# Weight sums added by GpSimd from two plain loads, and seven-product quads in two FFN down groups

## What is computed

```python
g = h2 @ w_gate;  u = h2 @ w_up              # 1024 -> 2816
x = x + (silu(g) * u) @ w_down               # first block's FFN
y = square(relu(h @ w_up)) @ w_down          # the two MLPs, 1024 -> 4096 -> 1024
mod = silu(c) @ ada_w + ada_b                # 112 rows of 128 values
```

## Time and profile before

| | us |
|---|---|
| median of 3 runs (lowest, highest) | 1738.54 (1738.35, 1739.76) |
| the profiled execution | 1739.29 |
| its span in the trace | 1737.4 |
| TensorE busy | 1713.6 |
| VectorE busy | 1254.3 |
| ScalarE busy | 685.2 |
| GpSimd busy | 120.1 |

### The profile page before, as it was taken

One profiled execution on the slowest core, in us unless ns is written; L12 is line 12 of the kernel. 1 busy time (PEld: TensorE's weight loads), 2 busy tenths in 40 slices (PEclk: granted clock), 3 DMA queues, 4 the chain that ended last, 5 costly groups with the idle time before them and its releaser, 6 DMA issues. The chain is left out here.

```text
span 1737.4 us, 23695 instructions
## 1 busy us (share of the span) xinstructions
PE 1713.6 (99%) x9000; PEld 1431.2 (82%) x9000; DVE 1254.3 (72%) x1869; ACT 685.2 (39%) x1051; POOL 120.1 (7%) x182
## 2 busy tenths in 40 slices
PE   9999999999999999999999999999999999999998
PEld 8777777888888888888898989887767889898987
DVE  7866555766666676877886868678675887777766
ACT  5236544322222253234544343344534453434341
POOL 0000000011011000100200000002000010000001
PEclk9999999999999999999999999999999999999999
DMA  7321112666566533653264646431411336364541
GB/s 253 106 97 38 43 55 67 199 207 229 193 206 229 193 110 112 234 179 118 63 178 126 183 131 185 166 121 49 139 49 40 107 94 172 98 170 107 163 167 49
DMA packets 67299, 235.77 MB, mean 136 GB/s; under 512 B 7808, under 2 KB 9984, under 8 KB 67008
## 3 DMA queue, kind: packets, MB, share of 16 engines
q1 hardware_dynamic: 46800, 161.24, 27.4%
q0 software_dynamic: 20112, 72.62, 15.2%
q10 hardware_dynamic: 288, 0.59, 0.1%
HBM read 231.55 MB, written 2.10 MB: 134 GB/s over the span
## 5 line engine op out<-in xcount | busy, mean ns | idle before, releaser
L1347 DVE TENSOR_TENSOR w_lo<-w_raw,w_hi 128x1024 fp32r<-128x1024 f32 x307 | 375.2, 1222 | 104.8 <-ACT w_hi L925 98.0
L925 ACT ACTIVATE w_hi<-w_raw 128x1024 fp32r<-128x1024 f32 x307 | 322.3, 1053 | 308.7 <-PE psum L2270 142.7
L2268 PE MATMUL psum<-h_hi,w_hi 128*128 128x512 f32 x1056 | 411.8, 390 | 0.0
L2269 PE MATMUL psum<-h_lo,w_hi 128*128 128x512 f32 x1056 | 410.9, 389 | 0.0
L2270 PE MATMUL psum<-h_hi,w_lo 128*128 128x512 f32 x1056 | 410.8, 389 | 0.0
L2268 PEld LDWEIGHTS psum<-h_hi,w_hi 128*128 128x128 f32 x1056 | 198.3, 188 | 41.7 <-issue 0.5
L2270 PEld LDWEIGHTS psum<-h_hi,w_lo 128*128 128x128 f32 x1056 | 198.2, 188 | 41.3
L2269 PEld LDWEIGHTS psum<-h_lo,w_hi 128*128 128x128 f32 x1056 | 198.3, 188 | 41.3 <-issue 0.5
L1358 DVE SCALAR_TENSOR_TENSOR ada_raw<-ada_raw,c_row 128x1024 f32<-128x1024 f32 x112 | 136.0, 1219 | 5.8 <-DMA ada_raw<-in_ada 5.8
L2268 PE MATMUL psum<-hid_hi,w_hi 128*128 128x512 f32 x344 | 133.8, 389 | 0.0
L2269 PE MATMUL psum<-hid_lo,w_hi 128*128 128x512 f32 x344 | 133.8, 389 | 0.0
(11 more groups left out here) (376 smaller groups left out, 2875.5 us busy)
## 6 DMA issues: line engine op xcount, KB each, us to landing
w_raw<-in_wstream SPq DMA_DIRECT2D x283, 512.0 KB, 4.1
ada_raw<-in_ada POOLq DMA_DIRECT2D x112, 512.0 KB, 4.0
w_diff<-in_wstream SPq DMA_DIRECT2D x12, 512.0 KB, 5.8
w_raw<-in_wstream POOLq DMA_DIRECT2D x12, 512.0 KB, 5.5
w_diff<-in_wstream POOLq DMA_DIRECT2D x12, 512.0 KB, 5.4
x<-in_xT SPq DMA_DIRECT2D x8, 256.0 KB, 5.4
outT<-x SPq DMA_DIRECT2D x16, 128.0 KB, 1.8
con<-in_consts SPq DMA_DIRECT2D x1, 1032.0 KB, 9.5
```

Source lines behind the costliest of these rows:

```text
L925: act.activation(w_hi[:, slot, :], w_raw[:, slot, :], ACT.Copy).then_inc(whi_done, 1)
L1347: dve.tensor_tensor(w_lo[:, slot, :], w_raw[:, slot, :], w_hi[:, slot, :].bitcast(F32), ALU.subtract).then_inc(wlo_done, 1)
L2268: pe.matmul(bank, w_hi[:, slot, w], hi[:, ra + k, :], start=k == 0, stop=False)
L2269: pe.matmul(bank, w_hi[:, slot, w], lo[:, ra + k, :], start=False, stop=False)
```

## The change

The sums A and D are added by GpSimd instructions: SyncE loads a21 into the slot and a22 into a new buffer w_part, GpSimd adds them (`first_sum`); SyncE loads only a21 into w_diff, and GpSimd adds a11, which lies in its ring slot anyway (`last_sum`). The slot of a11 is held until then (diff_made). Groups 0 and 1 of the FFN get quads on x, and their gate/up stages make the pair sums. Rows: the FFN's gate/up stages 13, 20, 13; each quads stage with rows has 2, one per quad behind unit D; the first MLP's up stages 0, 8, 8, 7. In a stage ahead of quads the last two blocks have no row. The scratch for GpSimd's descriptors is 4096 bytes, to make room for w_part.

```diff
-            inc.update(gate=nblk // 2, hi=nblk // 2, rhs=nblk // 2)
+            parts = nblk // 4 * 3 if about.get("paired") else nblk // 2
+            inc.update(gate=nblk // 2, hi=parts, rhs=parts, pair=nblk // 4 if about.get("paired") else 0)
...
-            gemm("gateup", 4, "h", h, kouter=AHEAD, summed=summed)
-            gemm("gateup", 12, "h", h, f0=2, rows=12)
+            gemm("gateup", 4, "h", h, kouter=AHEAD, summed=summed, paired=True)
+            gemm("gateup", 12, "h", h, f0=2, rows=13, paired=True)
         else:
-            gemm("gateup", 2 * nk, "h", h, rows=(0, 16, 12)[g])
+            gemm("gateup", 2 * nk, "h", h, rows=(0, 20, 13)[g], paired=g == 1)
         if g == 2:
             take("g_m0", "r_m0")
-        gemm("acc", 8, "hid", hid, nk=nk, dst="x", first=False, sq=False, twin=g == 2, rows=(12, 12, 0)[g])
+        if g < 2:
+            quads(hid, False, "x", 2)
+        else:
+            gemm("acc", 8, "hid", hid, nk=nk, dst="x", first=False, sq=False, twin=True)
...
-    mlp(h, (0, 4, 4, 7), (0, 0, 0, 0), "g_kv", "g_m1", "r_m1", fore=1, old="r_f0", paired=(0, 1, 2))
+    mlp(h, (0, 8, 8, 7), (2, 2, 2, 0), "g_kv", "g_m1", "r_m1", fore=1, old="r_f0", paired=(0, 1, 2))
...
+        w_part = sb("w_part", [P, D])
...
-            def load_sum(n, quad, follows):
+            def load_parts(n, quad, follows):
 
                 if follows:
                     sp.wait_ge(sum_made, 2 * quad - 1)
+                    sp.wait_ge(diff_made, quad)
                     sp.wait_ge(wlo_done, n - U_A - QUAD + U_A11 + 1)
                 else:
                     sp.wait_ge(wlo_done, n + 1 - RAW)
-                sp.dma_start(w_raw[:, n % RAW, :], wstream[SOURCE[n][1][0]]).then_inc(sum_begun, 16)
+                sp.dma_start(w_raw[:, n % RAW, :], wstream[SOURCE[n][1][0]]).then_inc(parts_loaded, 16)
+                if quad:
+                    before = last_of(U_A, n)
+                    sp.wait_ge(raw_loaded[before % RAW], 16 * (before // RAW + 1))
+                sp.dma_start(w_part[:, :], wstream[SOURCE[n][1][1]]).then_inc(parts_loaded, 16)
...
-                    sp.dma_start(w_diff[:, :], wstream[SOURCE[n + U_D - U_A][1][0]]).then_inc(diff_begun, 16)
+                    sp.dma_start(w_diff[:, :], wstream[SOURCE[n + U_D - U_A][1][1]]).then_inc(diff_loaded, 16)
...
                 elif SOURCE[n - RAW][0] is not None:
                     sp.wait_ge(sum_made, 2 * (SOURCE[n - RAW][2] + 1))
+                    sp.wait_ge(diff_made, SOURCE[n - RAW][2] + 1)
...
-            def weight_sums(n, k):
+            def first_sum(n, k):
 
                 slot = (n + U_A) % RAW
-                pool.wait_ge(sum_begun, 16 * (k + 1))
-                pool.dma_start(w_raw[:, slot, :], wstream[SOURCE[n + U_A][1][1]], accum_op=ALU.add).then_inc(sum_loaded, 16)
-                pool.wait_ge(sum_loaded, 16 * (k + 1))
-                pool.sem_inc(raw_loaded[slot], 16)
-                pool.wait_ge(diff_begun, 16 * (k + 1))
-                pool.dma_start(w_diff[:, :], wstream[SOURCE[n + U_D][1][1]], accum_op=ALU.add).then_inc(diff_loaded, 16)
+                pool.wait_ge(parts_loaded, 32 * (k + 1))
+                pool.tensor_tensor(w_raw[:, slot, :], w_raw[:, slot, :], w_part[:, :], ALU.add).then_inc(raw_loaded[slot], 16)
+
+            def last_sum(n, k):
+
+                m = n + U_A11
+                pool.wait_ge(diff_loaded, 16 * (k + 1))
+                pool.wait_ge(raw_loaded[m % RAW], 16 * (m // RAW + 1))
+                pool.tensor_tensor(w_diff[:, :], w_diff[:, :], w_raw[:, m % RAW, :], ALU.add).then_inc(diff_made, 1)
...
-                    upto = s["at"]["ada"] + s.get("rows", 0) * (s["nblk"] - AHEAD) // s["nblk"]
+                    upto = s["at"]["ada"] + s.get("rows", 0) * (s["nblk"] - AHEAD) // (s["nblk"] - 2)
...
-                    weight_sums(s["at"]["n"] + s["nblk"], s["at"]["quad"])
+                    first_sum(s["at"]["n"] + s["nblk"], s["at"]["quad"])
                 if s["kind"] == "quads":
-                    for q in range(1, QUADS):
-                        weight_sums(s["at"]["n"] + q * QUAD, s["at"]["quad"] + q)
+                    for q in range(QUADS):
+                        if q:
+                            first_sum(s["at"]["n"] + q * QUAD, s["at"]["quad"] + q)
+                        last_sum(s["at"]["n"] + q * QUAD, s["at"]["quad"] + q)
...
-                        act.wait_ge(diff_loaded, 16 * (quad + 1))
+                        act.wait_ge(diff_made, quad + 1)
...
-                    return y[:, 4 * Q + i:4 * Q + i + 3:2, half_of(h)]
+                    return (x if s["dst"] == "x" else y)[:, 4 * Q + i:4 * Q + i + 3:2, half_of(h)]
...
+                    if s["rows"] and u == U_D:
+                        weighted(s["at"]["ada"] + Q, s["at"]["ada"] + Q + 1)
...
                             dve.tensor_tensor(val, val, gate, ALU.mult).then_inc(gu_done, 1)
-                            lo_of(f)
+                            if not s.get("paired"):
+                                lo_of(f)
+                            elif t.b % 4 == 3:
+                                dve.wait_ge(gu_done, at_["gate"] + f + 1)
+                                pair_sums(s, at_["pair"] + t.b // 4)
+                                pair_lo(s, at_["hi"] + t.b // 4 * 3, (f + s.get("f0", 0)) // 2)
...
-                    weighted(at_["ada"] + t.b * rows // s["nblk"], at_["ada"] + (t.b + 1) * rows // s["nblk"])
+                    over = s["nblk"] - 2 if s.get("ahead") else s["nblk"]
+                    weighted(at_["ada"] + min(t.b, over) * rows // over, at_["ada"] + min(t.b + 1, over) * rows // over)
...
-    nc = bacc.Bacc("TRN2", target_bir_lowering=False, num_devices=1, dynamic_dma_scratch_size=8192)
+    nc = bacc.Bacc("TRN2", target_bir_lowering=False, num_devices=1, dynamic_dma_scratch_size=4096)
```

More of the change, by code:

```diff
@@ L162, in values, with quads @@
         add("values", dict(n=1, vs=0 if at == 3 else 1, o=4 if at == 3 else 0), group=group, slot=at, rhs="h")
-    def quads(hid, first, dst="y"):
-        add("quads", dict(n=QUADS * QUAD, o=QUADS * QUAD + REST, quad=QUADS), r0=hid, first=first, dst=dst)
+    def quads(hid, first, dst="y", rows=0):
+        add("quads", dict(n=QUADS * QUAD, o=QUADS * QUAD + REST, quad=QUADS, ada=rows), rows=rows, r0=hid, first=first, dst=dst)
     def filler(nblk, chunks, nk, nout, **about):
@@ L260, in mlp @@
             if g in paired:
-                quads(hid, g == 0)
+                quads(hid, g == 0, rows=down[g])
                 continue
@@ L447, in build @@
         y_at = place[0]
+        y_at = place[0]
         y = sb("y", [P, DT, S])
@@ L758, in build, with pair_sum_of @@
         rise_sq = [scratch[:, i, :] for i in (0, 1, 3, 4)]
+        def pair_sum_of(s):
+            return pair_sum_ffn if s["evac"] == "gateup" else pair_sum_mlp
         def last_of(unit, n):
@@ L995, in step @@
                         act.activation(gate, gate, ACT.Silu).then_inc(gate_done, 1)
-                    if evac == "gateup" and t.j % 2 == 1:
+                    if evac == "gateup" and s.get("paired"):
+                        if t.b % 4 == 3:
+                            act.wait_ge(gu_done, at_["gate"] + t.b // 2 + 1)
+                            pair_hi(s, at_["pair"] + t.b // 4, (t.b // 2 + s.get("f0", 0)) // 2)
+                    elif evac == "gateup" and t.j % 2 == 1:
                         act.wait_ge(gu_done, at_["gate"] + t.of(2) + 1)
@@ L1014, in step @@
                                 act.wait_ge(bank_free, BANKS + t.o + 1)
-                                pair_hi(at_["pair"] + t.b // 2, t.b // 2)
+                                pair_hi(s, at_["pair"] + t.b // 2, t.b // 2)
                             return
@@ L1439, in put, with pair_sums @@
                                              op1=ALU.mult).then_inc(bank_free, 1)
-            def pair_sums(p):
+            def pair_sums(s, p):
                 b11, b12, b21, b22 = (scratch[:, i, half_of(h)] for i in range(2) for h in range(2))
-                g3, g2, g4 = (pair_sum[:, i, :] for i in range(3))
+                g3, g2, g4 = (pair_sum_of(s)[:, i, :] for i in range(3))
                 dve.tensor_tensor(g3, b22, b12, ALU.subtract).then_inc(pair_step, 1)
@@ L1648, in step @@
                             dve.wait_ge(out_done, t.o + 1)
-                            dve.wait_ge(rhs_ready, at_["rhs"] + f)
+                            if s.get("paired"):
+                                val = scratch[:, t.b // 2 % 2, :]
+                                dve.wait_ge(rhs_ready, at_["rhs"] + t.b // 4 * 3)
+                            else:
+                                dve.wait_ge(rhs_ready, at_["rhs"] + f)
                             dve.tensor_tensor(val, bank, rstd[:, :], ALU.mult).then_inc(bank_free, 1)
@@ L1661, in step @@
                             dve.wait_ge(bank_free, BANKS + t.o + 1)
-                            pair_sums(at_["pair"] + i)
```

(6 more changed lines are left out.)

18 lines of the change are left out of this document (9 added, 9 removed).

## The result

The changed kernel takes **1762.29 us** (median of 4 runs, 1761.35 to 1764.08) against 1739.11 us (4 runs of the kernel before beside it, 1738.35 to 1739.76): a ratio of 1.0135, 95% interval 1.0117 to 1.0152. The forecast was 1743.0 with a range of 1728 to 1750: its sign was right, its size was not (23.2 us slower in place of 4.5). The profiled execution has a span of 1761.1 us, 23.7 more than before.

The account below looks back on a forecast made before the run. TensorE, busy 99% of the span, was taken as the bound, with VectorE the engine to watch. -6.4 - 3.0 + 10.8 + 1.5 + 1.6 = +4.5 us on the median 1738.54 gave 1743.0 us, range 1728 to 1750.

Parts of the forecast that it names:

- Part 2, rows spread: First MLP's groups 1 and 2: moving rows leaves the hid_lo wait, removes most waits for y; -3.0 us.
- Part 1, the products: Two FFN groups: 8 blocks become 14 units, 43.5 to 40.3 us each; -6.4 us.
- I cost it at nothing; the cover is 10 us of idle VectorE: FFN gate/up stages: added rows, pair sums and weight sums fit, VectorE busy 77 of 87 us; 0 us.
- rival (c): FFN products gain nothing because VectorE comes late to the quads; 1735.5 us; no chance of its own, with (b) 0.20.
- Part 3, the second quads' adds: Quads stages: GpSimd adds hold VectorE; first sums +10.8 us over eight stages, difference adds +1.5 over five.
- The upper end of the price: GpSimd add beside a two-SBUF-input VectorE operation: the later waits, up to 2.4 us (bounds 0 and 2.4).
- (a): GpSimd adds cost VectorE nothing; only -6.4 and -3.0 stand, 1729.1 us; chance 0.30.
- (b): Half price: parts land behind w_lo in all eight stages, 0.8 us each; 1735.5 us; chance with (c) 0.20.
- Part 3, the first quads' adds: Up stages of groups 1 and 2: GpSimd adds hold VectorE, 0.8 us each; +1.6 us.
- Elsewhere the first quad's adds fall 12 us ahead of the stage into slack: Stages outside groups 1 and 2: the first quad's adds cost nothing.
- its worst case, every hold at its high end: All VectorE holds at 15.2 + 12 + 4.8 us: 1761 us, needing VectorE to have no slack anywhere.
- What would show it: Signs: TensorE waits of 0.8 to 2 us per stage; VectorE's ada_raw wait in gate/up if rows come too fast.

Follow-up runs that it names:

- e2: The changed kernel with both GpSimd adds left out, waits and loads kept, sums wrong: 1733.70 us, ratio 0.9976.
- e8: e1, but GpSimd no longer waits for the first sum's transfer to land; ScalarE passes the semaphore on: 1736.95 us, ratio 0.9998.
- e10: The changed kernel with fewer rows ahead of quads (FFN gate/up 13, 14, 19) and e8's accumulating transfers: 1733.49 us, ratio 0.9964.
- e6: The changed kernel with only the GpSimd adds of each stage's second quad, the first quad's left out: 1747.01 us, ratio 1.0056.
- e3: The kernel before with the sums made by GpSimd adds as its only change: 1751.93 us, ratio 1.0089.
- e5: The changed kernel with only the GpSimd adds of each stage's first quad, the second quad's left out: 1755.41 us, ratio 1.0108.
- e12: The changed kernel with each GpSimd add replaced by three memsets, which read nothing from SBUF; sums left out: 1735.11 us, ratio 0.9988.
- e1: The changed kernel with its sums made by accumulating transfers again, as in the kernel before: 1746.33 us, ratio 1.0050.

## Why the prediction was wrong

**Part 2, rows spread, -3.0 us: right.** Groups 1 and 2 of the first MLP take 42.1 and 41.9 us in e2 against 43.8 and 43.3: -3.0; in e8, with right sums, 42.0 each. The wait for hid_lo stayed (1.5 and 1.4 us), the waits for y went, as worked out.

**Part 1, the products, -6.4 us: half right.** In e2 the FFN's two groups take 41.3 and 42.5 us, so 3.2 us came of 6.4. Of the missing 3.2, 3.0 are waits in the gaps between starts, for hid_lo of the last block (0.7 and 2.0 us as the view of waits counts them). The step that failed is "I cost it at nothing; the cover is 10 us of idle VectorE". VectorE is idle for 17 us in group 1's gate/up stage of e2, but not where it counts. At its end:

```profile
487.79 0.68 DVE L1673 TENSOR_TENSOR scratch<-psum,rstd 128x512 f32<-128x512 f32 x1
490.12 1.23 DVE L1372 TENSOR_TENSOR w_lo<-w_raw,w_hi 128x1024 fp32r<-128x1024 f32 x1 [1.65 <-ACT w_hi L946]
...
494.23 0.69 DVE L1681 TENSOR_TENSOR scratch<-psum,rstd 128x512 f32<-128x512 f32 x1 [0.21 <-DVE w_raw L1496]
```

Two rows come just ahead of 487.79. ScalarE makes w_hi only behind its activation of that block, so VectorE is idle for 1.65 us; then a w_lo and the two weight sums follow one another, and the last block is evaluated 2.5 us behind TensorE's start (491.72). With 14 rows in place of 20 (e10) it is 1.3 us behind, and the group takes 41.3 us. This is the mechanism of rival (c), a VectorE that comes late with its rows and pair sums, to which the text gave no chance of its own.

**Part 3, the second quads' adds, +10.8 and +1.5: nearly right.** Alone (e6) they cost 13.3 us in the medians and 15.5 in the stages, 2.3 of that by the clock. The upper end of the price was the true one: the later operation waits for whatever is left of the earlier one, up to the add's 2.4 us. The two orders cost waits of 2.0 and 0.7 us as against 1.9 and 0.8, and which of them a stage meets can hang on hundredths of a microsecond. Rivals (a) and (b) fall with e2, e3 and e6.

**Part 3, the first quads' adds, +1.6: wrong, and the bulk of the miss.** Alone (e5) they cost 21.7 us. Two sentences failed. "Elsewhere the first quad's adds fall 12 us ahead of the stage into slack": these are six stages, and in four of them the adds that hold VectorE fall 9 to 15 us ahead, where there is no slack: over e2 they lose 3.2 and 1.5 us in the FFN and 4.2 and 2.6 in the first group of each MLP, which has no row ahead of it. Only in the last two, with the adds 16 to 19 us ahead, was there slack (0.2 and 0.1 us lost). And for groups 1 and 2 the text said that no room is left and then took a third of a hold each, 0.8 us; alone the adds cost 5.8 and 6.4 us there, 3.3 and 3.7 of it as longer waits for hid_lo against holds of 3.5 and 3.9, the rest as half-rate spacing. In the changed kernel those two stages lost 3.5 and 4.6 us against before, part 2's gain included. The bounds were drawn per stage from one hold of 2.4; the trace has two adds there, each of which can hold.

**Not in the sum: the clock.** Of the 29.3 us that the adds cost in the stages (e2 to the changed kernel), 22.0 are waits and 7.3 are half-rate spacing behind them. Nothing in the forecast priced a wait at more than its length. That its worst case, every hold at its high end, came to 1761, near the measured time, is luck: it has nothing for the clock, nothing for part 1's loss, and nothing for the first quads' adds in those four stages.

**Overlap.** The costs of e5 and e6 don't add up: 24.0 + 15.5 in the stages against 29.3. In the last two stages the second quad's first add comes 7.1 and 6.2 us into the stage with both quads' adds, behind w_lo, and 5.6 and 5.5 us in e6, ahead of it: 1.0 us lost in place of 2.0. That is some 2.3 of the 10.2 us; where the rest of the overlap comes from, and why the add comes later, was not tried.

**What would show it.** The sign named for rows that come too fast, VectorE's wait for ada_raw in the gate/up stages, did appear (none before, 8.9 us after in those of the FFN's groups 0 and 1; 5.8 and 13.2 us in the whole trace), but e12 has it as high in all (13.5) at 1735 us: it is not a sign of the adds' loss. What such waits cost shows in e1 and e8. TensorE's waits of 0.8 to 2 us for y are in e6; in the changed kernel waits of 2.2 to 4.8 us for hid_lo stand in their place.

## What to carry to other kernels

An add moved from DMA to an idle GpSimd is paid for by VectorE, whenever VectorE has two SBUF inputs beside it: count such a meeting at what is left of the add when VectorE's operation comes, the add's full length at worst, and set against it only idle time of VectorE in those very microseconds, not in the stage's mean. Here the end of the stage that hands over to TensorE is where the in-order VectorE had least to give; the adds that fell 16 us and more ahead cost next to nothing. No run moved the adds to earlier blocks, so that this would repair the others is not shown. Don't leave a wait for a landing in a queue in front of other loads. A wait of TensorE can cost more than its length, since the clock may be at its lower level behind it.
